# Head of the even mixer: identity products first, a row product ahead of the transposes, two panels in halves, the k panel ahead of two ada panels

## What is computed

```python
c_act = silu(c)                                             # c: (1, 1024)
mod = (c_act @ ada_w[l] + ada_b[l]).reshape(1, 6, 1, 1024)   # ada_w[l]: 1024 x 6144
sh1, sc1, g1, sh2, sc2, g2 = (mod[:, i] for i in range(6))
h = rms_norm(x, norm1_g[l]) * (1.0 + sc1) + sh1
proj = h @ w_in                                             # w_in: 1024 x 2560
u, v, q, k, vd = split_cols(proj, (512,) * 5)
a_out = spatial_gating(gelu(u), gelu(v), ln_g, ln_b, w_s, b_s)  # layer norm of v, causal 128x128 w_s
b_out = differential_attention(q, k, vd, lam, subln_g, lam_init) # lam from the small vectors lq, lk
x = x + g1 * (concatenate([a_out, b_out]) @ w_out)
h = rms_norm(x, norm2_g[l]) * (1.0 + sc2) + sh2
x = x + g2 * grouped_moe(h, router_w, router_b, w_gu[l], w_down[l])
```

## Time and profile before

| | us |
|---|---|
| median of three runs | 904.07 (901.06 to 904.52) |
| profiled execution, span from first to last instruction | 902.5 |
| PE busy (matmuls) | 809.5 (90%) |
| DVE busy | 327.1 (36%) |
| ACT busy | 162.6 (18%) |
| HBM read | 292.18 MB, 325 GB/s over the span |

### The profile page before, as it was taken

One profiled execution on the slowest core, in us unless ns is written; L12 is line 12 of the kernel. 1 busy time (PEld: TensorE's weight loads), 2 busy tenths in 40 slices (PEclk: granted clock), 3 DMA queues, 4 the chain that ended last, 5 costly groups with the idle time before them and its releaser, 6 DMA issues.

```text
span 902.5 us, 11955 instructions
## 1 busy us (share of the span) xinstructions
PE 809.5 (90%) x4950; PEld 408.7 (45%) x4950; DVE 327.1 (36%) x813; ACT 162.6 (18%) x397; POOL 23.9 (3%) x65
## 2 busy tenths in 40 slices
PE   4998999999999899856999999898999999899864
PEld 2575444454333332212767778764454333332211
DVE  1187441472111111102689565535472211110102
ACT  2031231411001100001101333432411011100001
POOL 2000010110000000000000000000100000000000
PEclk9998999999999999978999999999999999999988
DMA  9999998697899999999999425202988899999994
GB/s 348 389 387 387 361 340 311 235 380 275 306 411 409 409 410 410 409 409 393 387 338 330 175 94 187 95 1 78 412 321 293 314 410 409 409 408 410 409 409 167
DMA packets 96348, 294.08 MB, mean 326 GB/s; under 512 B 2720, under 2 KB 3360, under 8 KB 96288
## 3 DMA queue, kind: packets, MB, share of 16 engines
q1 hardware_dynamic: 95584, 290.62, 84.0%
q10 hardware_dynamic: 560, 2.10, 0.6%
q0 software_dynamic: 144, 0.52, 0.1%
HBM read 292.18 MB, written 1.05 MB: 325 GB/s over the span
## 4 chain that ended last, share of the span: by engine, by line
PE 52%; issue 24%; SPq 10%; DVE 5%; DMA 4%; ACT 3%; POOL 0%; DVEq 0%; POOLq 0%; ACTq 0%
PE bank L823 14%; PE bank L819 12%; SPq L497 10%; PE bank L1060 8%; PE bank L1082 3%; DMA ring<-w_gu_dram 3%; PE bank L1046 2%; PE bank L711 2%; PE bank L735 2%; PE bank L1097 1%; PE bank L680 1%; DMA ring<-ada_w_dram 1%; PE bank L890 1%; PE bank L698 1%; PE bank L726 1%
## 5 line engine op out<-in xcount | busy, mean ns | idle before, releaser
L1060 PE MATMUL bank<-ring,scr 128*64 128x512 f32 (+1 forms) x1024 | 196.8, 632 | 36.7 <-DMA ring<-w_gu_dram 23.2
L823 PE MATMUL bank<-hT,ring 128*128 128x256 f32 x640 | 142.0, 381 | 0.8 <-DVE hT L1607 0.8
L1060 PEld LDWEIGHTS bank<-ring,scr 128*64 128x64 f32 (+1 forms) x1024 | 56.4, 132 | 164.4 <-issue 131.8
L823 PEld LDWEIGHTS bank<-hT,ring 128*128 128x128 f32 x640 | 120.5, 190 | 18.3 <-issue 2.0
L1082 PE MATMUL bank<-ring,scr 128*64 128x512 f32 (+1 forms) x544 | 102.2, 597 | 3.4 <-DMA ring<-w_down_dram 3.0
L2030 DVE TENSOR_TENSOR hT<-bank,gb 128x512 f32<-128x512 f32 x28 | 19.4, 692 | 195.0 <-PE bank L1082 195.0
L819 PE MATMUL bank<-ring,xh 128*128 128x512 f32 x128 | 58.7, 612 | 0.7 <-ACT xh L1260 0.7
L819 PE MATMUL bank<-ring,hT 128*128 128x512 f32 x128 | 58.1, 610 | 0.6 <-ACT hT L1292 0.5
L1082 PEld LDWEIGHTS bank<-ring,scr 128*64 128x64 f32 (+1 forms) x544 | 29.7, 127 | 61.4 <-issue 56.2
L1445 ACT ACTIVATE scr<-bank 128x256 f32<-128x256 f32 (+1 forms) x42 | 19.1, 454 | 212.9 <-PE bank L1071 123.4
L1097 PE MATMUL bank<-hT,scr 64*128 64x512 f32 x224 | 55.6, 615 | 1.8 <-DVE hT L2030 1.8
(11 more groups left out here) (249 smaller groups left out, 662.2 us busy)
## 6 DMA issues: line engine op xcount, KB each, us to landing
ring<-w_gu_dram SPq DMA_DIRECT2D x60, 2048.0 KB, 21.0
ring<-w_down_dram SPq DMA_DIRECT2D x28, 2048.0 KB, 19.0
ring<-ada_w_dram SPq DMA_DIRECT2D x24, 2048.0 KB, 15.8
ring<-od_w_in_dram SPq DMA_DIRECT2D x9, 2048.0 KB, 15.8
ring<-ev_w_in_dram SPq DMA_DIRECT2D x5, 2048.0 KB, 19.5
ring<-w_down_dram SPq DMA_DIRECT2D x8, 1024.0 KB, 18.9
scr<-w_gu_dram SPq DMA_DIRECT2D x10, 512.0 KB, 5.6
ring<-ev_w_out_dram SPq DMA_DIRECT2D x2, 2048.0 KB, 16.6
```

Source lines behind the costliest of these rows:

```text
L823: ins = pe.matmul(banks[h][:, m * 256:(m + 1) * 256], w[:, c, (2 * h + m) * P:(2 * h + m + 1) * P], x_part[:, c, :], start=(c == 0 and m = ...
L1060: ins = pe.matmul(b[o:o + r, :].rearrange("p (u f) -> p u f", u=2), h[:, c, r * i:r * i + r], wm, start=(first and c == 0), stop=(last and ...
```

## The change

It puts five identity products (`keep_busy(5)`) ahead of everything else on PE; moves the first row product ahead of the 16 transposes, and drops the one identity product behind it; loads the panels of v and q of layer 0 in two transfers of 1024 KB each, of which the first counts up a semaphore of its own (`upper_in`), so that fills 0 and 2 wait for the chunks 0 to 3 alone and fills 1 and 3 for the rest; and puts the k panel ahead of the ada panels 4 and 5 in the order of loads. The two side loads now hang on positions 6 and 7, which are k and ada 4.

```diff
@@ -162,7 +162,7 @@
 FIRST_ADA = [0, 2, 1, 3]
-PRE = [[("ada", 0), ("ada", 2), ("in", "v"), ("in", "q"), ("ada", 1), ("ada", 3), ("ada", 4), ("ada", 5), ("in", "k"),
+PRE = [[("ada", 0), ("ada", 2), ("in", "v"), ("in", "q"), ("ada", 1), ("ada", 3), ("in", "k"), ("ada", 4), ("ada", 5),
         ("in", "vd"), ("ada", 6), ("ada", 7), ("ada", 8), ("ada", 9), ("in", "u"), ("ada", 10), ("ada", 11),
         ("out", 0), ("out", 1)],
@@ -399,6 +399,7 @@
         front_done, half_in = sem("front_done"), sem("half_in")
+        upper_in = {"v": sem("upper_in_v"), "q": sem("upper_in_q")}
@@ -506,10 +507,14 @@
-                    load(pl, panel(pl.slot), src, PRE_AT[l] + k >= PANELS)
-                    if l == 0 and k == 4:
+                    if l == 0 and n in upper_in:
+                        sp.dma_start(panel(pl.slot)[:, 0:4, :], src[:, 0:4, :]).then_inc(upper_in[n], 16)
+                        sp.dma_start(panel(pl.slot)[:, 4:8, :], src[:, 4:8, :]).then_inc(panel_in[pl.slot], 16)
+                    else:
+                        load(pl, panel(pl.slot), src, PRE_AT[l] + k >= PANELS)
+                    if l == 0 and k == 6:
                         sp.dma_start(sgw, sgu_w[0].rearrange("g t s -> t g s")).then_inc(sguw_in, 16)
-                    if l == 0 and k == 5:
+                    if l == 0 and k == 7:
                         sp.dma_start(row, rows.partition_broadcast(P)).then_inc(rows_in, 16)
                         sp.dma_start(rb_row[:, :], router_b.partition_broadcast(P)).then_inc(rb_in, 16)
@@ -804,7 +809,9 @@
-                if f % 2 == 0:
+                if l == 0 and name in upper_in:
+                    pe.wait_ge(*((panel_in[pl.slot], pl.landed) if f % 2 else (upper_in[name], 16)))
+                elif f % 2 == 0:
                     pe.wait_ge(panel_in[pl.slot], pl.landed)
@@ -1228,13 +1235,15 @@
             pe.wait_ge(consts, 2)
-            norm_T(0)
+            keep_busy(5)
             pe.wait_ge(cact_ready, 1)
             pe.wait_ge(part_ready, 1)
-            for n in (0, 1):
-                ada_row(n)
-                keep_busy(1)
-                ada_row_sum(n)
+            ada_row(0)
+            norm_T(0)
+            ada_row_sum(0)
+            ada_row(1)
+            keep_busy(1)
+            ada_row_sum(1)
             keep_busy(1)
             even()
```

## The result

The changed kernel takes 905.39 us (median of 20 runs, 903.83 to 907.58), the kernel before 901.95 us (20 runs, 897.94 to 904.70). The ratio is 1.0038, 95% interval 1.0026 to 1.0050: slower by 3.4 us (2.3 to 4.5), with an increase of 4.0 us forecast.

The account below looks back on a forecast made before the run. Load order was taken to bound the first 90 us or so, PE's own work from some 95 us. DVE's ada(6) moves from 69.86 to 73.9, and this +4.0 on the median 904.07 gives 908.1 us; range 902 to 912.

Parts of the forecast that it names:

- The sum: Main case: DVE starts ada(6) 4.0 us later, PE restarts at 80.0, delay passes to the end; 908.1 us, chance 0.52.
- the restart: PE's sum of ada 5, waiting for DVE's ada_out(4) behind ada(6); forecast at 80.0 instead of 75.98 us.
- The head: Start through first fill of v: identity products, early row product, halves; fill 0.8 to 2.2 us earlier, lost waiting for ada 3.
- Landings: Times when loaded panels and side loads arrive, from their bytes at 387 GB/s in the new order; split priced at 0.
- Wait (1): PE idle 3.4 us for masked sgu_w until 47.05, ahead of v's second half; clock loss up to 3.0 us.
- Wait (2): DVE's first wait in even(), for the parameter rows: 53.5 instead of 47.90 us, delaying ada(4) through ada_out(4).
- The rival of the clock: PE's pause before 80 stays under 2 us, clock stays at 2.4 GHz, 3.0 us saved: +1.0, 905.1 us; chance 0.22.

Follow-up runs that it names:

- 1: Changed kernel with load order and places of both side loads as before, leaving identity products, early row product and halved v and q; 0.9995 of the kernel before, 901.81 us.
- 2: Changed kernel with side loads back at k == 4 and k == 5, k panel still ahead of ada 4 and 5; 1.0052 of the kernel before, 906.59 us.
- 3: Kernel before with only k ahead of ada 4 and 5 and side loads at positions 6 and 7; 1.0032 of the kernel before, 905.53 us.
- Number 4: Kernel before with two identity products in PE's pause ahead of the sum of ada 5; 0.9980 of the kernel before, 900.22 us.
- 8: Changed kernel with three identity products added in PE's wait for the masked sgu_w; 1.0134 of the kernel before, 915.40 us.
- 6: Changed kernel with PE loosened from DVE's ada folds, old panel order, both side loads at k == 5; 0.9990 of the kernel before, 900.66 us.
- 9: Changed kernel with three identity products before sgu_w and two instead of five at the start; 1.0058 of the kernel before, 906.61 us.
- number 7: Changed kernel with PE loosened from DVE's ada folds, its own order, side loads at k == 4 and k == 5; 1.0003 of the kernel before, 903.01 us.

## Why the prediction was right

- **Direction and size.** 908.1 against 904.07 were forecast, +4.0; measured were +3.4 (2.3 to 4.5). Against the median of 20 runs the same sum gives 906.0. The chance of 0.59 for within 0.5% was the right one of the three.
- **What of it was luck.** The sum passes the restart's delay on whole and lets the clock fall in both kernels. The profiled pair does neither: the restart is 4.4 us late, and at 139 us nothing of that is left. That the medians differ by 3.4 is shown, and by 1, 2 and 3 that the order does it; that it is the delay of 4.4 less some spared falls of the clock fits, but no run splits it so.
- **The head**: the first fill was forecast 0.8 to 2.2 us earlier, and it is 2.1 in this pair; some 0.5 to 1.1 us of that are the slow start of the profiled execution of before (22.97 to 23.61 in the other kernels with the old head). Its worth of nothing is shown by 1 and 3.
- **Landings**: ada 3 was put at 40.2, sgu_w at 46.3, ada 4 at 51.7, the rows at 53.5, ada 6 at 72.6; they come at about 40.5 (PE's row product at 40.66), 46.5, 51.9, 53.7 and 72.4. The split of v and q showed no price (40.66 with it and 40.64 without, see 3). The Trainium skill's page "DMA: Bandwidth & Descriptors", section "Anatomy of one DMA", has a fixed part of about 2.0 us for each DMA on GpSimd's path. The DMAs here are issued by SP, and in this full queue no such part is paid in series.
- **Wait (1)**, put at 3.4 us up to 47.05: 3.36 us up to 47.27. The fall of the clock behind it, put at up to 3.0 us, came: the fill is 2.0 us longer and q's slot is free at 64.25 (64.8 at worst). **Wait (2)**: L1710 at 53.80 (53.5 forecast), ada(6) at 74.22 (73.9), restart at 80.34 (80.0).
- **The step that was told wrongly** is the cause of wait (2). I named the rows' index as what makes DVE late, and had ada 4's own delay of one panel in the list of landings without using it. Number 2 shows that moving k is enough: with the rows in time DVE waits for ada 4 until 53.85. The late rows stand only 0.65 us behind it. Whoever had mended the indices on the strength of my text would have won nothing in the time.
- **The rival of the clock** (0.22, no second fall) is what the profiled execution of after shows. In the runs the difference of 3.4 lies between that rival's +1.0 and the sum's +4.0, nearer to the sum. Number 4 puts a price of 1.9 us (0.6 to 3.1) on the average over executions for that fall. How often it falls in either kernel without a profile can't be read from the runs.
- **The chain of 8** I had not foreseen anywhere: a price for adding instructions to PE that lies 380 us behind the place where they are added.

## What to carry to other kernels

Where the DMA queue is full, a panel moved ahead delays each one that it passes by its own bytes; ask who reads the passed ones first, and look up every side load that is tied to a position in the list. A head start is worth what the next landing allows. If two engines meet at one semaphore, look whether the waiting one has other work that can be put ahead of it: here that was worth 0.3 to 0.4%, where no order of loads tried won anything that can be told from none, and took away the pause in which the clock fell. Part of it is the clock's: filling the pause with identity products alone was worth 0.2%. And before a kernel is judged by its profile, take several of the same stretch: the first fill of v lies at 22.97 to 24.11 with the same head.

## What was not expected of the hardware

- PE's stop behind the branch of the overflow code, 4.8 to 4.9 us in all kernels, with a second one of 4.44 us when six records were added ahead of it, 0.8 to 0.9 us in numbers 1, 6 and 9, 0.28 in number 7, and none visible in the changed kernel and number 2. Numbers 1, 2, 6, 7, 9 and the changed kernel all have 4958 records, so the count alone does not set the length. The DMA records show the rest. Number 8, DMA queues in the windows 425.9 to 427.1 and 431.8 to 433.1 us (from 427.1 to 431.8 this queue moves nothing):

```profile
q8 instruction: 1, 0.02, 5.5%
...
q8 instruction: 1, 0.02, 5.3%
```

  These are two transfers of 16 KB on a queue for instructions. They end at 427.0 and 433.0 us, and PE goes on at 428.61 and 434.28. In all twelve profiles PE's first record behind the branch starts 1.6 us behind the end of the first transfer, and the second transfer ends some 6 us behind the first. In the six kernels with 4958 records the eighth record behind the branch starts 1.3 to 1.5 us behind the end of the second (429.52 and 430.93 in number 1); in number 8, with six records more ahead, it is the second record, and 4.44 of the 6 us between the transfers are idle. How long the seven records ahead take depends on the clock (1.06 us each at 1.2 GHz, 0.59 at 2.4 in these traces), and that is why the same count shows a stop of 0 to 0.9 us. All this fits PE waiting there for its code; no run changed the transfers themselves. That they are late because the other queues fill the DMA engines (share 1.05 in those windows) was only argued.
- The kernel before spreads over 6.8 us in 20 runs (897.94 to 904.70), about 0.75%. Two profiles of the same stretch differ by one or two falls of the clock of 1.7 to 3 us each, so a single profiled pair (0.7 us here) can't carry a verdict on a change of this size.
- In the profile before, the clock fell at a pause of 2.3 us (the window of 75 to 80 at 0.56); with 1.95 us in the changed kernel and 1.78 in number 3 it did not, and in numbers 2, 8 and 9 it fell at pauses of 4.04, 3.72 and 4.48 us. It also fell within fills, behind waits of 1.7, 0.9 and 0.6 us with small matmuls between them (number 1, at 46.4).
